# The opening of a two-block inference kernel: constant products on TensorE, a third row block, and the first rounding on VectorE

## The reference, cut to what matters

```
c_act = silu(c)                                   # 1024 numbers
mod   = c_act @ w_mod + b_mod                     # shift, scale (and gate), 1024 each
h     = rms_norm(x, g_norm) * (1 + scale) + shift # 256 x 1024
proj  = h @ w_in                                  # 1024 x 8192, split in eight parts
```

## Time and profile before

| | us |
|---|---|
| median of 3 runs | 1424.07 (1423.84 to 1424.59) |
| profiled execution, its own time | 1424.62 |
| span of that execution | 1422.8 |
| TensorE busy | 1406.1 |
| VectorE busy | 959.2 |
| ScalarE busy | 746.0 |

### The profile page before, as it was taken

The page is one execution under the profiler, slowest core; times in us unless marked ns, Lnnn a source line. Parts: engine busy times, 40 slices in busy tenths (PEclk is TensorE's granted clock), DMA queues, the critical chain, the costliest instruction groups (busy, mean ns, idle before and its releaser), DMA issues.

```text
span 1422.8 us, 18171 instructions
## 1 busy us (share of the span) xinstructions
PE 1406.1 (99%) x7038; PEld 1184.3 (83%) x7038; DVE 959.2 (67%) x917; ACT 746.0 (52%) x785; POOL 74.1 (5%) x91
## 2 busy tenths in 40 slices
PE   7999999999999999999999999999999999999997
PEld 6888888888888888888888888888888878888886
DVE  6879686786774666776774686764874446677736
ACT  3774766545553557655543565543534445555434
POOL 0000000010000100110000010000202101000000
PEclk9999999999999999999999999999999999999999
DMA  9747454466455553464555374555453633655541
GB/s 394 301 152 275 173 175 172 163 227 225 177 192 193 193 199 118 149 219 166 187 195 217 153 278 162 181 198 217 176 208 120 233 121 143 227 177 181 203 178 45
DMA packets 40388, 272.62 MB, mean 192 GB/s; under 512 B 4609, under 2 KB 5505, under 8 KB 8706
## 3 DMA queue, kind: packets, MB, share of 16 engines
q1 hardware_dynamic: 36864, 261.65, 50.2%
q10 hardware_dynamic: 3458, 10.04, 2.3%
HBM read 270.62 MB, written 1.05 MB: 191 GB/s over the span
## 4 chain that ended last, share of the span: by engine, by line
PE 96%; DMA 1%; ACT 1%; DVE 1%; issue 0%; SPq 0%; DVEq 0%; ACTq 0%; POOLq 0%; POOL 0%
PE acc L2190 20%; PE acc L2191 20%; PE acc L2505 19%; PE acc L2202 10%; PE acc L2510 10%; PE acc L2228 10%; PE turn L2256 3%; DMA mod_raw<-in_units 1%; DMA raw<-in_units 1%; PE turn L2405 0%; PE aux L2786 0%; ACT whi L431 0%; PE aux L2331 0%; PE aux L2658 0%; DVE gate_part L1717 0%
## 5 line engine op out<-in xcount | busy, mean ns | idle before, releaser
L1236 DVE TENSOR_TENSOR wlo<-raw,whi 128x2048 fp32r<-128x2048 f32 x233 | 532.9, 2295 | 156.0 <-ACT whi L431 155.7
L431 ACT ACTIVATE whi<-raw 128x2048 fp32r<-128x2048 f32 x233 | 445.0, 1915 | 220.1 <-PE acc L2228 106.6
L2190 PE MATMUL acc<-whi,feeds 128*128 128x512 f32 (+1 forms) x872 | 347.2, 399 | 0.0
L2191 PE MATMUL acc<-whi,feeds 128*128 128x512 f32 (+1 forms) x872 | 338.8, 389 | 0.0
L2505 PE MATMUL acc<-feeds,whi 128*128 128x512 f32 x1152 | 314.7, 395 | 0.0
L2505 PEld LDWEIGHTS acc<-feeds,whi 128*128 128x128 f32 x1152 | 197.1, 189 | 26.5
L2510 PEld LDWEIGHTS acc<-feeds,wlo 128*128 128x128 f32 x1152 | 176.6, 189 | 24.7
L2190 PEld LDWEIGHTS acc<-whi,feeds 128*128 128x128 f32 x872 | 164.5, 189 | 35.5 <-issue 2.1
L2191 PEld LDWEIGHTS acc<-whi,feeds 128*128 128x128 f32 x872 | 164.6, 189 | 32.3 <-issue 0.7
L2510 PE MATMUL acc<-feeds,wlo 128*128 128x256 f32 x1152 | 183.2, 281 | 0.0
L2202 PE MATMUL acc<-wlo,feeds 128*128 128x512 f32 x648 | 174.2, 391 | 0.0
(11 more groups left out here) (367 smaller groups left out, 1230.4 us busy)
## 6 DMA issues: line engine op xcount, KB each, us to landing
raw<-in_units SPq DMA_DIRECT2D x237, 1024.0 KB, 4.8
mod_raw<-in_units SPq DMA_DIRECT2D x6, 1024.0 KB, 10.7
gpost<-in_norm_g ACTq DMA_DIRECT2D x8, 512.0 KB, 4.6
gpre<-in_norm_g ACTq DMA_DIRECT2D x6, 512.0 KB, 7.1
mod_more<-in_units SPq DMA_DIRECT2D x2, 1024.0 KB, 23.2
h<-in_x SPq DMA_DIRECT2D x2, 512.0 KB, 10.1
w_ax<-in_w_ax SPq DMA_DIRECT2D x1, 1024.0 KB, 26.6
bgate<-in_b_gate SPq DMA_DIRECT2D x1, 1024.0 KB, 27.9
```

The costliest lines, as they stand in the source:

```text
L431: act.activation(whi[:, u % RING, :], raw[:, u % RING, :], ACT.Copy).then_inc(hi_ready, 1)
L1236: dve.tensor_tensor(wlo[:, u % RING, :], raw[:, u % RING, :], whi[:, u % RING, :].bitcast(F32), ALU.subtract).then_inc(lo_ready, 1)
L2190: pe.matmul(out, xh, wh, start=first, stop=False)
L2191: pe.matmul(out, xl, wh, start=False, stop=False)
```

## The change

TensorE multiplies a constant tile of ones (`paced()`, 128 x 128 by 128 x 128, the result goes to a part of PSUM that is overwritten later): twelve times at the start, once after every second of the one-column products of its first two row blocks, and four, three and eight times between later steps. It takes a third row block (r = 4) of half 0 from VectorE. Its block for half 1 moves from ahead of unit 0 to between the two token halves of unit 0. VectorE rounds unit 0 itself, after `mod_ended(0)`, so ScalarE's first rounding goes and ScalarE starts with `first_feed(0, 0)`. VectorE forms the rest of unit 0's weights behind `first_rest(0, 0)` and no longer ahead of it.

```diff
-MOD_PE = ((0, 2), (0,))
-MOD_DVE = ((1, 3, 4, 5, 6, 7), (1, 2, 3, 4, 5, 6, 7))
+MOD_PE = ((0, 2, 4), (0,))
+MOD_DVE = ((1, 3, 5, 6, 7), (1, 2, 3, 4, 5, 6, 7))
...
-                        act.wait_ge(mod_columns, min(u + 1, 2))
+                        act.wait_ge(mod_columns, min(u + 1, 3))
...
             square_sum(h[:, 1, :], xn[:, 1, :])
-            hi()
+            n["u"] += 1
             first_feed(0, 0)
             first_feed(0, 1)
+            act.wait_ge(hi_ready, 1)
             hi(2)
...
             mod_ended(0)
+            dve.wait_ge(loaded[0], 16)
+            dve.wait_ge(mod_columns, 1)
+            dve.tensor_copy(whi[:, 0, :], raw[:, 0, :]).then_inc(hi_ready, 1)
+            first_rest(0, 0)
             lo()
-            first_rest(0, 0)
             mod_products(1, MOD_DVE[1][0:1])
...
-            def mod_column(half, i):
+            def mod_column(half, i, pace=0):
...
+                    if pace and f % pace == 1:
+                        paced(1)
...
+            def paced(count):
+
+                for _ in range(count):
+                    pe.matmul(acc[1][:, BANK:BANK + P], ones[:, :], ones[:, :], start=True, stop=True)
+
             pe.wait_ge(pads_ready, 1)
+            paced(12)
             pe.wait_ge(c_ready, 1)
-            mod_column(0, 0)
-            mod_column(0, 1)
+            mod_column(0, 0, 2)
+            mod_column(0, 1, 2)
+            paced(4)
+            mod_column(0, 2)
             first_turns(0, 0)
+            paced(3)
             mod_sums(0)
             first_turns(0, 1)
-            pe.wait_ge(columns_read, 1)
-            mod_column(1, 0)
+            paced(8)
             for t in range(TOK):
                 pe.wait_ge(first_fed, t + 1)
                 unit(0, t)
                 ends(wide(0, 0, t), t, False)
+                if t == 0:
+                    pe.wait_ge(columns_read, 1)
+                    mod_column(1, 0)
```

More of the change, by code:

```diff
@@ L1368, in mod_begun @@
                 for i in range(len(MOD_PE[half])):
-                    at = 2 * KC * half + KC * i
+                    at = 4 * KC * half + KC * i
                     ins = dve.tensor_tensor(by_kind(mod[:, :], half),
@@ L2318, in mod_column @@
                 for f in range(KC):
-                    at = 2 * KC * half + KC * i + f
+                    at = 4 * KC * half + KC * i + f
                     last = pe.matmul(aux[:, 0, at:at + 1], mod_source(half, r)[:, P * f:P * f + P], c_act[:, r:r + 1],
                                      start=True, stop=True)
+                    if pace and f % pace == 1:
+                        paced(1)
                 last.then_inc(mod_columns, 1)
```

## The result

The changed kernel takes 1428.78 us (median of 9 runs, 1424.28 to 1429.78) against 1424.15 us before (9 runs on the same chip, 1423.58 to 1425.77). The ratio is 1.0023, 95% interval 1.0015 to 1.0032: slower by 4.6 us, where no change was forecast and the range ended at 1426.0. The profiled execution took 1428.98 us, 4.4 more than the one of before.

A forecast was written before the change was run, and what follows sets the result against it. TensorE, busy 1406.1 of 1422.8 us, was taken as the bound. Unit 2's 0.9 us gain becomes a wait at 49.1 behind unit 4's load: +0.9 - 0.9 = 0, forecast 1424.0 us, range 1422.9 to 1426.0.

The forecast's parts named there:

- Constant products, the clock: TensorE's opening: constants raise the clock by 6 to 8 us, the first twelve cost nothing, TensorE is early for VectorE's sum.
- Rival (c): TensorE's opening: clock rises and falls again between 12.4 and 22.8; unit 2 near 43.9, +2.8 us, 1426.9; chance 0.08.
- Rival (b): TensorE's opening: clock doesn't rise, TensorE late from the start; unit 2 near 48.3, +7.3 us, 1431.3; chance 0.05.
- Third row block: Half 0: VectorE loses one 1.3 us product, its sum taken at 17.86; TensorE's third column costs 1.7 us.
- ScalarE feeds first, VectorE rounds: Unit 0: feed 19.85 to 22.1 hides VectorE's 1.3 us rounding; unit 0 starts at 22.8 instead of 24.84.
- Half 1 and unit 2: VectorE gains 1.45, loses 1.25 in rounding and waiting; unit 2 starts at 40.1 instead of 41.03, 0.9 us left.
- The pin at 46.7 and 49.1: Unit 4's load lands at 46.6 as before; ScalarE's copy holds the transposes to 49.12, turning 0.9 us into a wait.
- Rival (a): Transposes near 49.1: ScalarE's copy doesn't hold them or unit 4 lands earlier; TensorE keeps 0.9 us, 1423.2; chance 0.07.
- Rival (d): Unit 4's load lands as much later as it is issued later, 1.5 us: 1425.5; chance 0.05.
- the forecast's lead of 0.9 us: TensorE at unit 2: start at 40.1 instead of 41.03, what is left of more than 2 us.

The follow-up runs named there:

- e8: Changed kernel, third row block kept on TensorE, with constant products denser, one behind every one-column product: 1424.25 us.
- e1: Changed kernel without any of the constant products, all else as changed: 1424.75 us.
- e4: Changed kernel with unit 0 rounded by ScalarE again and VectorE's subtraction of unit 0 ahead of `first_rest(0, 0)`: 1426.34 us.
- e3: Changed kernel with the third row block back on VectorE: 1424.91 us.
- e9: Kernel before without six `wlo` products of units 2 and 3 at t = 0, so part of the computation is left out: 1423.86 us.
- e10: e9 with unit 4's load issued early, ahead of the tables: 1422.84 us.
- e5: Changed kernel with the third row block back on VectorE and denser constant products, two behind each product of the first two columns: 1424.36 us.
- e12: Kernel before with 40 one-column bfloat16 products added on TensorE in the first 5 us: 1424.67 us.
- e11: e5 with its constant products made wide, one of up to 512 columns for up to four of 128: 1424.80 us.
- e6: e5 with unit 4 loaded ahead of the four tables: 1424.60 us.
- e2: Kernel before with constant products alone, none ahead of unit 0: 1425.31 us.

## Why the prediction was wrong

By its own steps:

**Constant products, the clock: wrong, the step that failed.** "I take it that they do, by 6 to 8 us" held until 10.7 us, and what was built on it was that the level would stay. It fell while TensorE ran two one-column products (0.37 us) and one constant product (0.30 us) in turn, without a gap, and stayed down for 17 us, through columns, transposes, sums, ten further constant products and most of the eight ahead of unit 0. Rival (c) had this mechanism at a chance of 0.08, but mis-sized: it put the fall at 12.4 and paid the constant products at the upper level, so its `mod_sums(0)` ended at 21.6, its unit 2 began at 43.9 and its time was 1426.9. Measured were 24.5, 46.16 and 1428.8. Rival (b) is out, since the clock did rise. In the forecast's sum `mod_sums(0)` could start at 15.3; it started at 21.06. Of these 5.8 us the largest term is the constants' own: 15 of them stand ahead of `mod_sums(0)`, 3.3 us by the forecast, 6.2 by the timeline. The three columns took 7.3 instead of 5.0, and the rest is a start at 6.64 instead of 6.3 and the slower transposes. As cover for a wait they were free only if TensorE was early; once the clock was down they were TensorE's own lateness. That the fall is the cause, and not the moved work by itself, is shown by e8 (more constants, no fall, 1424.25) and by e1 (none, 1424.75). The runs of the changed kernel and of e4, which split by their clock, agree with it. What sets in a run whether the clock falls stays open.

**Third row block: right in its part, wrong in its price.** VectorE's half-0 sum was ready for TensorE at 18.08 (17.86 forecast). On TensorE the column cost 3.3 us at the lower level (15.62 to 18.89) instead of 1.7, and e3 shows that without it 0.8 of the 4.6 us is left.

**ScalarE feeds first, VectorE rounds: right.** The rounding took 1.23 us, near the value taken (1.3) and far from the upper bound of 2.28. The Trainium skill, "VectorE: DVE Perf Modes", section "Mode 2×_2P", gives the copy double rate in float32; 1.23 us beside 2.28 for the two-source subtraction of the same size agrees, for the rounded destination too. ScalarE's feed hid it from TensorE: the rest waited 1.22 us for it. The loss of 1.25 us in half 1 was measured as 1.4 by e4 against the changed kernel.

**Half 1 and unit 2: the mechanism was right, from a wrong start.** `scale_g` came 3.65 late. From there to unit 2 the order added 1.4, the slack at `mod_sums(1)` took back 0.6, and the second fall, which no case of mine had, added 0.64. The prediction's 0.35 us of room ahead of unit 2 wasn't there: in e8 VectorE's 0.46 reached the transposes whole.

**The pin at 46.7 and 49.1: right,** and shown by e9 and e10. It swallows gains up to unit 4's landing and lets losses through, and the changed kernel came 5.1 us late to it. Rival (a) is refuted by e9. Rival (d) is refuted by the issues: unit 4 was issued at 23.60 before, at 26.44 in e1, 26.53 in e5 and 30.31 in the changed kernel, and took 23.0, 20.0, 20.2 and 16.2 us to land, so it landed at 46.4 to 46.7 in all four, though the last was issued 6.7 us later than the first.

**What no case had: the loads.** The forecast took every landing from the trace of before. More instructions on TensorE bring its instruction fetch forward among the loads of the opening, and with it went delays of up to 1.7 us at x rows 128 to 255 (e5) and 1.1 us at half 1's mod blocks (e12). In the changed kernel TensorE was later than any load, so this isn't in its 4.6 us; but with the clock up (e8) it is what left the end of `scale_g` at 20.80 where the forecast had 19.8. Where `scale_g` did come early (19.48 in e3, 19.77 in e11), half 1 waited for a mod block until 27.5. In no trace of e1, e3, e5, e6, e8 and e11, which all have VectorE round unit 0, did unit 2 start ahead of the 41.03 of before (41.09 in e6 was the earliest), and the forecast's lead of 0.9 us never came about. That e8 lands at 1424.25, close to the forecast of 1424.0, is therefore in part luck: there was no lead for the pin to swallow.

The clock went 1.00, 0.50, 1.00, 0.50 in the rows of the changed kernel, and TensorE had no idle time between 1.19 us and the end of unit 0. The Trainium skill, "TensorE: Matmul & The Clock Gate", section "HAM oscillation", which the prediction gave to rival (c), tells of such falls where TensorE waits for data between bursts of products. The shape is the same, but not the cause: the first fall here came in the midst of unbroken one-column and constant products. By the page's rule read strictly the clock would have held, and the time would have been near the forecast, so here the measurement decides.

## What to carry to other kernels

Filler work that is to hold TensorE's clock up is on TensorE's own path wherever real work stands behind it: price it at the lower level too, and look in the trace whether the level holds through the mixed stretch before putting anything else on the strength of it. Find the next pin downstream (here a load, at 49.1) first, and prove it by making the engine early in some cheap way: if it is real, the early work can only lose. Instructions added to an engine move its fetches, and a fetch among loads that others wait for can cost a microsecond where the added work costs nothing.

## What the runs showed of the hardware

- With a constant 128 x 128 float32 product behind every second one-column product the clock fell near 10.7 us in the changed kernel, 10.0 in e2, 10.5 in e3 and 8.8 in e4; with one behind every product (e8), or two (e5), it stayed at 1.00 from 7 to 45 us.
- The fall isn't the same in every run of one program: nine runs of the changed kernel had mean clocks of 0.992 to 0.995, eleven of e4 0.991 to 0.997, and the time followed. In e3 (0.993 to 0.996) it didn't.
- The granted-clock column reads 1.00 for stretches ahead of the first change that is recorded: in e1, at 7 to 15 us, where one-column passes take 0.21 us, the lower level's time. The durations decide there.
- One 16 KB instruction fetch (q8), moved among the opening's loads, went with one of them landing 1.3 to 1.7 us later (unit 0 at 20.00 instead of 18.66 in e2, x rows at 17.89 instead of 16.17 in e5).
